# Where the tiles behind the small ones begin in a two-layer transformer kernel

## What is computed

```python
def first_block(x, c, ...):
    shift1, scale1, gate1, shift2, scale2, gate2 = jnp.split(silu(c) @ w_ada + b_ada, 6, axis=-1)
    h = rms_norm(x, norm1_g) * (1.0 + scale1) + shift1
    qa, ka, va, qb, kb, vb, qi, ki, wi, gates = jnp.split(h @ w_in, SPLITS, axis=-1)
    y_a = dsa_sparse_attention(rms_norm(qa), rms_norm(ka), va, qi, ki, wi)
    lam = exp(sum(lam_q1 * lam_k1)) - exp(sum(lam_q2 * lam_k2)) + lambda_init
    y_b = differential_attention(rms_norm(qb), rms_norm(kb), vb, lam, subln_g, lambda_init)
    x = x + gate1 * ((g_a * (y_a @ w_up_a) + g_b * (y_b @ w_up_b)) @ w_o)
    h2 = rms_norm(x, norm2_g) * (1.0 + scale2) + shift2
    return x + gate2 * ((silu(h2 @ w_ff1) * (h2 @ w_ff3)) @ w_ff2)

def second_block(x, p, positions, ...):
    rq, rk, rv, rg, cq, ckv, krope, gr, gm = split(rms_norm(x) @ w_in)
    a_ret = (rms_norm(retention(rope(rq), rope(rk), rv)) * silu(rg)) @ w_br
    a_mla = latent_attention(cq, ckv, krope, pos) @ w_bm
    x = x + (sigmoid(gr) * a_ret + sigmoid(gm) * a_mla) @ w_o
    x = x + square(relu(rms_norm(x) @ w_up)) @ w_down
    return x + sigmoid(rms_norm(x) @ w_ple_gate) * (p @ w_ple)
```

## Time and profile before

| | us |
|---|---|
| median of 3 runs | 1987.8 |
| lowest and highest run | 1986.4, 1987.96 |
| the profiled execution: span from the first to the last instruction | 1986.2 |
| TensorE busy | 1959.3 |
| VectorE busy | 1066.4 |
| ScalarE busy | 807.1 |
| GpSimd busy | 117.8 |

### The profile page before, as it was taken

How to read it: one execution, slowest core, us unless ns; L and a number is a source line. 1 busy time by engine, 2 the same in 40 slices (tenths; PEclk the granted TensorE clock), 3 DMA queues, 4 the chain that set the end, 5 groups by cost and what they waited for, 6 DMA issues and landing times.

```text
span 1986.2 us, 24265 instructions
## 1 busy us (share of the span) xinstructions
PE 1959.3 (99%) x9224; PEld 1603.9 (81%) x9224; DVE 1066.4 (54%) x1695; ACT 807.1 (41%) x1358; POOL 117.8 (6%) x138
## 2 busy tenths in 40 slices
PE   7999999999999999999999999999999999999998
PEld 6778777888888888888888888878888888888887
DVE  5687877456343543475545454466654463434354
ACT  5343555634222233343232323587742342322343
POOL 3140000002000000200000000000000200000010
PEclk9999999999999999999999999999999999999999
DMA  9842212122333432322222222211232432323321
GB/s 364 328 172 85 64 50 100 64 86 71 105 90 87 114 90 79 111 85 85 85 85 84 85 84 74 66 55 49 61 95 97 132 101 88 104 93 97 100 91 64
DMA packets 196579, 199.64 MB, mean 101 GB/s; under 512 B 7548, under 2 KB 170449, under 8 KB 194065
## 3 DMA queue, kind: packets, MB, share of 16 engines
q1 hardware_dynamic: 192416, 175.15, 28.4%
q0 software_dynamic: 4080, 23.40, 3.0%
HBM read 194.33 MB, written 4.19 MB: 100 GB/s over the span
## 4 chain that ended last, share of the span: by engine, by line
PE 93%; DVE 3%; ACT 3%; issue 1%; DMA 1%; SPq 0%; DVEq 0%; ACTq 0%
PE bank L774 47%; PE bank L1281 4%; PE bank L1027 4%; PE bank L739 4%; PE bank L864 4%; PE bank L850 3%; PE bank L1541 3%; PE bank L1353 2%; PE bank L1082 2%; PE bank L1011 1%; PE bank L894 1%; PE bank L1259 1%; PE bank L977 1%; PE bank L1270 1%; PE bank L1301 1%; PE bank L1217 1%
## 5 line engine op out<-in xcount | busy, mean ns | idle before, releaser
L1657 ACT ACTIVATE w_hi<-raw 128x2048 fp32r<-128x2048 f32 (+4 forms) x164 | 283.2, 1728 | 405.5 <-PE bank L774 296.3
L2423 DVE TENSOR_TENSOR w_lo<-raw,w_hi 128x2048 fp32r<-128x2048 f32 (+4 forms) x163 | 336.8, 2067 | 147.7 <-ACT w_hi L1657 145.8
L774 PE MATMUL bank<-h_hi,w_hi 128*128 128x512 f32 x864 | 337.6, 391 | 0.0
L774 PE MATMUL bank<-h_hi,w_lo 128*128 128x512 f32 x864 | 336.3, 389 | 0.0
L774 PE MATMUL bank<-h_lo,w_hi 128*128 128x512 f32 x864 | 336.2, 389 | 0.0
L774 PEld LDWEIGHTS bank<-h_hi,w_hi 128*128 128x128 f32 x864 | 162.2, 188 | 34.1 <-issue 0.5
L774 PEld LDWEIGHTS bank<-h_lo,w_hi 128*128 128x128 f32 x864 | 162.2, 188 | 34.1 <-issue 0.5
L774 PEld LDWEIGHTS bank<-h_hi,w_lo 128*128 128x128 f32 x864 | 162.2, 188 | 34.0
L774 PE MATMUL bank<-u_hi,w_hi 128*128 128x512 f32 x256 | 100.9, 394 | 0.0
L774 PE MATMUL bank<-u_hi,w_lo 128*128 128x512 f32 x256 | 100.4, 392 | 0.0
L774 PE MATMUL bank<-u_lo,w_hi 128*128 128x512 f32 x256 | 99.4, 388 | 0.0
(11 more groups left out here) (581 smaller groups left out, 4153.1 us busy)
## 6 DMA issues: line engine op xcount, KB each, us to landing
raw<-in_w_in SPq DMA_DIRECT2D x49, 1024.0 KB
raw<-in_w_ff SPq DMA_DIRECT2D x44, 512.0 KB
raw<-in_w_up SPq DMA_DIRECT2D x16, 1024.0 KB
raw<-in_w_down SPq DMA_DIRECT2D x16, 1024.0 KB
raw<-in_w_o SPq DMA_DIRECT2D x8, 1024.0 KB
raw<-in_w_br SPq DMA_DIRECT2D x8, 1024.0 KB
raw<-in_w_in SPq DMA_DIRECT2D x13, 512.0 KB
raw<-in_w_ff SPq DMA_DIRECT2D x8, 768.0 KB
```

The lines of the kernel that those rows point to most:

```text
L774: last = nc.tensor.matmul(dst, a, b, start=k == n == 0, stop=k == last_k and n == 2)
L1657: nc.scalar.activation(w_hi[:, slot, 0:width], raw[:, slot, 0:width], ACT.Copy).then_inc(hi_done, 1)
L2423: v.tensor_tensor(w_lo[:, slot, 0:width], raw[:, slot, 0:width], w_hi[:, slot, 0:width].bitcast(F32), ALU.subtract).then_inc(lo_done, 1)
```

## The change

Two fillers that nobody reads are put in: `to_wide` (64 bytes per partition) behind `warm`, the last of the small tiles, and `to_wide_1` (160 bytes) behind the first layer's small ones. `junk` moves ahead of `qstat`, next to `att`; `ple_b` moves ahead of `vrows`; and `ldot` is no longer a tile but a view of `lrow`, so that the two products of the lambda vectors are written over their first factors. The tiles that began at 448, 288 and 320 modulo 512 then begin at 0. `xT`, `raw`, `w_hi`, `w_lo`, `h_hi` and `h_lo` stay at 128.

```diff
         warm = sbuf("warm", [P, 16])
+        sbuf("to_wide", [P, 16])
...
         att = sbuf("att", [P, 256], at=layer1)
+        junk = sbuf("junk", [P, 2, P], at=layer1)
         qstat = sbuf("qstat", [P, 2, 3, 8], at=layer1)
         qscale = sbuf("qscale", [P, 2, 8], at=layer1)
         wi = sbuf("wi", [P, QT, H_I], at=layer1)
         top8 = sbuf("top8", [P, 8], at=layer1)
-        junk = sbuf("junk", [P, 2, P], at=layer1)
+        sbuf("to_wide_1", [P, 40], at=layer1)
         start = ExitStack()
         x_in = sbuf("x_in", [P, QT, D], at=start)
         xnT = sbuf("xnT", [P, KD, S], at=start)
         ada_w = sbuf("ada_w", [P, 2, UW], at=start)
+        ple_b = sbuf("ple_b", [P, 4, S], at=start)
         vrows = sbuf("vrows", [P, P], at=start)
         crow = xT[0:KD, 0, 0:P]
         lrow = sbuf("lrow", [1, 4 * D_A], at=start)
-        ldot = sbuf("ldot", [1, 2, D_A], at=start)
+        ldot = lrow[:].rearrange("o (n two d) -> o n two d", n=2, two=2)[:, :, 0, :]
         lsum = sbuf("lsum", [1, 8], at=start)
-        ple_b = sbuf("ple_b", [P, 4, S], at=start)
         start.close()
```

## The result

The changed kernel takes 1994.24 us (median of 6 runs, 1994.0 to 1994.4), the kernel before 1987.1 (6 runs of the same chip, 1986.2 to 1988.0): ratio 1.0035, 95% interval 1.0024 to 1.0046. Forecast were 1981.9 and a gain of 5.9; measured is a loss of 7.1. The time lies in the range given, on the other side of zero: rival 2, at 0.25, is what happened.

A forecast was written before the change was run, and what follows sets the result against it. TensorE, 99% busy, was taken as the bound through its start-to-start matmul time; 4.5 us from 2016 matmuls and 1.4 from y's 192 made -5.9, so 1987.8 became 1981.9 us, range 1979.5 to 1995.0.

The forecast's parts named there:

- rival 2: Moved tiles meet the weights worse, interference repeating every 256 bytes: up to +8.7 us, 1996.5 us; chance 0.25.
- What bounds the kernel, and where the price lies: TensorE, 99% busy: price is the start-to-start time of 2016 matmuls at 228.9 ns and 192 at 234.2.
- Two reads at a distance: On TensorE, streamed and loaded operands are read at once and interfere by the distance of their starts: 226.7 to 234.2 ns.
- on the circle its two neighbours are the good ones, and I take the lower end: Moved tiles at distance 384, between 320 (228.9 ns) and 512 (as 0, 226.7), were put at 226.7: -5.9 us.
- 0 and 128 are both multiples of 128: Added reason for 226.7 ns with moved tiles at 0 and weights at 128, whereas 448 and 288 are not such multiples.
- the shorter way on the circle: The only argument named against a 256-byte period, under which distance 384 would give 231.2 to 233.3 ns.
- the straight line from 320 to 512: Interpolated matmul pitch at distance 384: 227.8 ns, a gain of 3.4 us.
- rival 1: Moved tiles' matmuls keep a middling pitch, 227.8 to 230 ns: 1984.4 to 1989.2 us; chance 0.29.
- Latent products: 240 matmuls streaming w against loaded latents, distance 192 to 128: 0.5 us either way, kept for the range.
- VectorE and ScalarE: Their reads and writes of moved tiles cost the same at three residues: 0.
- DMA: Loads into moved tiles, on the path at the first modulation weights' 13.23 us wait: 0, with 0.8 us both ways.
- The base: Differences worked out on the profiled execution, span 1986.2 us, and carried to the three runs' median of 1987.8.

## Why the prediction was wrong

- **What bounds the kernel, and where the price lies:** right. The pitch of some 2000 matmuls made the time; the groups' +9.0 us are larger than the whole difference, and nothing else grew.
- **Two reads at a distance:** right, and shown with the weights moved: h slowed to 233.3 without moving. That the load and the stream disturb each other while both read is inferred from the places; no run took the load away.
- **The step that failed: "on the circle its two neighbours are the good ones, and I take the lower end".** It had two assumptions. The first was that the circle is 512 bytes round; it is 256, so 384 is 128, and its neighbours, 96 and 160, are bad ones (233.4 and 234.2); u and g at 384 stood at 233.3 and not at 226.7. The second was that the pitch is smooth between neighbours; it isn't, 32 bytes from the best place it is at 233.4. The added argument, that 0 and 128 are both multiples of 128, is worth nothing either: they would have to be equal modulo 256. Nothing in the four distances told a period of 512 from one of 256, as the text itself says under rival 2; the preference came from "the shorter way on the circle" alone.
- **A slip beside it:** on the straight line from 320 to 512 the distance 384 lies a third of the way along and not half. The line gives 228.2 ns and a gain of 2.6 us, not 227.8 and 3.4; the forecast did not use it, only the lower end of rival 1 did.
- **Rival 2's price:** +8.7 at its end, with u, g, yr, m2 and mo at 233.3. They came to that: 3.31 + 2.30 + 1.61 + 0.85 + 0.65 = 8.7. y gave back 0.3 where 0.2 was written. un, left out with a word, added 0.35. Between traces with the same clock at the start the difference was 7.7: the groups' +9.0, less 0.6 at the start and some 0.7 in small groups.
- **Latent products:** 0.24 of the 0.5 kept for them. **VectorE and ScalarE:** 0, as written. **DMA:** taken at 0 with 0.8 both ways; it was 0.2 to 0.45 of gain on the path, and the rates by place that go with it could not be seen in the 7.2 and 6.7 us of the earlier trace rows.
- **The base:** the trace of before was one with the clock down behind the wait at 18 us, that of the change was not. The 40 slices of the earlier trace rows are some 50 us long each and do not show it. A comparison of the two spans alone would have put 1.6 us of that down to the fillers.

## What to carry to other kernels

Where 128x512 products in float32r follow each other without a wait, each with a load of its own (no other type or shape was measured here), let the streamed and the loaded operand begin at the same residue modulo 256 bytes; which residue doesn't matter for TensorE, and a multiple of 256 went with the faster transfers too. Aligning one side alone can be worse than leaving both: here it cost 7 us, and giving both one residue gained 7. Look at the distance from start to start, not at the busy time, and when some distances are known and one isn't, measure that one before it is interpolated.

## What was not expected of the hardware

- The pitch of one shape at one clock depends on the distance of two starts modulo 256: 226.7 ns at 0, 228.9 at 64, 232.3 to 234.3 at all other multiples of 32. Why 64 is milder than 32 or 192, no run tells.
- At one distance there can be two pitches: 64 gave 229.1 and 233.2 in one run, 384 gave 233.3 (u) and 232.3 (y). What chooses between them stays open, beyond that the slow one at 64 followed a stretch with the same pitch.
- With the tiles of the first stage at multiples of 256 bytes the transfers between 17 and 33 us ran at 408 to 412 GB/s, with none of them there at 387 to 391, some 5% less.
- Behind a wait of 2.0 us or more ahead of the products on x TensorE's granted clock fell in ten traces, behind the one of 0.8 us it did not; the drop costs some 1.6 us in this kernel.
